# Loads of the last stage behind the overflow block's weights, one input copy less

## What is computed

```python
u = rmsnorm(h, norm_ffn)
# top-1 group of 4, top-2 of the 4 experts in it: 2 of 16 experts per token
for e in range(N_EXPERTS):
    gu = jnp.einsum('bld,df->blf', u, w_gate_up[e])
    hid = jax.nn.silu(gu[..., :D_EXPERT]) * gu[..., D_EXPERT:]
    moe = moe + combine[..., e:e + 1] * jnp.einsum('blf,fd->bld', hid, w_down[e])
h = h + moe
u = rmsnorm(h, norm_ple)
gate = jax.nn.sigmoid(jnp.einsum('bld,de->ble', u, w_ple_gate))
h = h + gate * jnp.einsum('blp,pd->bld', p_l, w_ple_proj)
# then a final RMSNorm
```

## Time and profile before

| what | value |
|---|---|
| runs | 850.77, 850.83, 851.63 us, median 850.83 us |
| the profiled execution | 849.0 us, span 847.2 us |
| mean granted clock of PE | 0.994 |
| busy: PE, DVE, ACT, POOL | 822.9, 385.5, 215.2, 152.6 us |
| moved by DMA | 135.31 MB |

### The profile page before, as it was taken

One profiled execution on the slowest core, in us unless ns is written; L12 is line 12 of the kernel. 1 busy time (PEld: TensorE's weight loads), 2 busy tenths in 40 slices (PEclk: granted clock), 3 DMA queues, 4 the chain that ended last, 5 costly groups with the idle time before them and its releaser, 6 DMA issues. The chain is left out here.

```text
span 847.2 us, 13448 instructions
## 1 busy us (share of the span) xinstructions
PE 822.9 (97%) x5462; PEld 519.9 (61%) x5462; DVE 385.5 (46%) x857; ACT 215.2 (25%) x464; POOL 152.6 (18%) x184
## 2 busy tenths in 40 slices
PE   8999999999999999999999999999999999979996
PEld 4546777888889987777777775455343333334452
DVE  3223556676646522664852559546441111105543
ACT  3202153258223311131001101123031111114554
POOL 0234420014054133300220052001000000004000
PEclk9999999999999999999999999999999999989999
DMA  9420344402020110522252024005899999966111
GB/s 361 193 99 25 133 150 163 155 1 108 1 101 4 45 58 13 198 72 99 100 198 100 1 100 178 25 26 209 352 415 417 427 421 420 406 279 198 50 38 50
DMA packets 19197, 135.31 MB, mean 160 GB/s; under 512 B 2496, under 2 KB 3136, under 8 KB 11712
## 3 DMA queue, kind: packets, MB, share of 16 engines
q1 hardware_dynamic: 11888, 104.33, 31.2%
q0 software_dynamic: 4896, 24.48, 7.8%
q10 hardware_dynamic: 2352, 5.64, 2.0%
HBM read 119.01 MB, written 19.63 MB: 164 GB/s over the span
## 5 line engine op out<-in xcount | busy, mean ns | idle before, releaser
L765 PE MATMUL pair<-mem 128*128 128x288 f32 x640 | 158.9, 408 | 0.0
L765 PEld LDWEIGHTS pair<-mem 128*128 128x128 f32 x640 | 120.3, 190 | 35.6 <-ACT mem L1381 2.1
L935 PE MATMUL single<-mem 128*128 128x288 f32 x448 | 110.0, 407 | 0.3
L935 PEld LDWEIGHTS single<-mem 128*128 128x128 f32 x448 | 84.7, 190 | 25.7 <-issue 1.6
L1275 PE MATMUL single<-mem 128*32 128x512 f32 x768 | 85.1, 594 | 1.1 <-DVE mem L2304 0.9
L1381 ACT ACTIVATE mem<-single 128x256 f32<-128x256 f32 (+5 forms) x111 | 45.6, 421 | 134.7 <-PE single L1181 48.7
L1381 ACT ACTIVATE mem<-pair 128x512 f32<-128x512 f32 (+5 forms) x77 | 33.5, 485 | 156.7 <-PE pair L765 63.0
L1360 PE MATMUL pair<-mem 128*128 128x512 f32 (+1 forms) x192 | 63.3, 524 | 0.0
L1275 PEld LDWEIGHTS single<-mem 128*32 128x32 f32 x768 | 24.0, 110 | 52.7 <-issue 51.6
L2297 DVE SCALAR_TENSOR_TENSOR mem<-single,mem 128x256 f32<-128x256 f32 x12 | 5.8, 484 | 104.3 <-PE single L1275 91.4
L1172 PE MATMUL pair<-mem 128*128 128x512 f32 x112 | 51.0, 601 | 0.0
(11 more groups left out here) (407 smaller groups left out, 1135.2 us busy)
## 6 DMA issues: line engine op xcount, KB each, us to landing
mem<-in_w_gu SPq DMA_DIRECT2D x17, 2048.0 KB, 14.8
mem<-in_w_down SPq DMA_DIRECT2D x17, 1024.0 KB, 14.9
y_slots<-mem SPq DMA_DIRECT2D x12, 512.0 KB, 11.1
y_slots<-in_zeros POOLq DMA_DIRECT2D x8, 512.0 KB, 7.8
mem<-in_w_ga SPq DMA_DIRECT2D x2, 2048.0 KB, 7.6
mem<-in_w_gb SPq DMA_DIRECT2D x2, 2048.0 KB, 7.6
mem<-in_w_wo SPq DMA_DIRECT2D x2, 2048.0 KB, 7.7
mem<-in_w_pg SPq DMA_DIRECT2D x2, 2048.0 KB, 14.1
```

The lines of the kernel that those rows point to most:

```text
L765: last = nc.tensor.matmul(pb[:, hf, 0:HALF], w(k), rhs[:, k, hf * HALF:(hf + 1) * HALF], start=(k == 0), stop=(k == kk - 1))
L935: last = nc.tensor.matmul(single[plan.buf[s]][:, 0:HALF], lhs[:, k, :], rhs[:, k, :], start=(k == 0 and j in (0, 1, 3, 4)), stop=(k == 3), ...
```

## The change

The load of `w_pg0` and that of `w_proj` are taken out of SP's loop over phases. Both are issued behind the overflow block's pair of loads, with the load of `pT` between them, which moves from POOL's queue to SP's. The second copy of the last columns of `pT` goes away, and with it the two waits and the view that it had; tile 4 reads the first copy. `w_proj` and `pT` share the semaphore `ld_p`, on which PE waits once, for both.

```diff
-        pT4 = view(BLK + 17408, 2, 64)
...
-                if p == NPH - 2:
-                    sp.dma_start(view(BLK, CHUNK_W), a["w_pg0"]).then_inc(sem("w_pg"), 16)
                 if p:
                     store(p - 1)
                 for e in range(NEXP - 4):
                     if last_phase(e) == p - 1:
                         load_dn(e + 4)
-                if p == NPH - 3:
-                    sp.dma_start(w_proj.rearrange("p k c -> p (k c)"), a["w_proj"]).then_inc(sem("w_proj"), 16)
...
                     sp.dma_start(w_gu_flat[0], a["w_gu"][bass.ds(e * P, P), :]).then_inc(sem("ov_w"), 16)
                     sp.dma_start(w_dn_flat[0], a["w_down"][bass.ds(e * P, P), :]).then_inc(sem("ov_w"), 16)
+            sp.dma_start(w_proj.rearrange("p k c -> p (k c)"), a["w_proj"]).then_inc(sem("ld_p"), 16)
+            sp.wait_ge(sem("xT_mm"), NPH)
+            sp.dma_start(pT, a["pT"]).then_inc(sem("ld_p"), 16)
+            sp.dma_start(view(BLK, CHUNK_W), a["w_pg0"]).then_inc(sem("w_pg"), 16)
             store(NPH - 2)
...
-            pe.wait_ge(sem("ld_p"), 16)
-            pe.wait_ge(sem("w_proj"), 16)
+            pe.wait_ge(sem("ld_p"), 32)
...
-                if t == 4:
-                    pe.wait_ge(sem("ld_p"), 32)
...
-                            last = nc.tensor.matmul(pair[t % 2][rows, hf, cols], pT[:, k, t * P:t * P + n] if t < 4 else pT4[:, k, :],
+                            last = nc.tensor.matmul(pair[t % 2][rows, hf, cols], pT[:, k, t * P:t * P + n],
...
-            pool.wait_ge(sem("xT_mm"), NPH)
-            pool.dma_start(pT, a["pT"]).then_inc(sem("ld_p"), 16)
...
-            pool.wait_ge(sem("ld_p"), 16)
-            pool.dma_start(pT4, a["pT"][:, :, 4 * P:TOK]).then_inc(sem("ld_p"), 16)
```

## The result

| | before | after |
|---|---|---|
| median | 850.8 us (12 runs, 848.07 to 852.69) | 852.95 us (12 runs, 851.16 to 854.39) |
| ratio to before | | 1.0028, 95% interval 1.0017 to 1.004 |
| profiled execution, span | 849.0, 847.2 us | 853.86, 852.0 us |
| busy PE | 822.9 us | 825.1 us |

The change made the kernel slower by 0.28%: 2.4 us by the ratio, while the two medians are 2.15 us apart. The forecast was 849.6 us in a range from 847.5 to 851.6. The before column holds twelve runs; the median of 850.83 us that the forecast started from is that of three of them.

The account below looks back on a forecast made before the run. The prediction took PE as the bound, with time to regain only at its 4.09 us wait for the overflow weights and the clock fall behind it. Terms -2.7 + 1.5 = -1.2 us gave 849.6 us, range 847.5 to 851.6.

Parts of the forecast that it names:

- Step 1: Overflow pair lands by 742.7, its products start 3.6 us earlier, and PE finishes the projections at 764.25 to 765.95, was 770.80.
- Step 2: Loads moved behind the overflow pair land later but stay hidden; w_proj and pT have 3.5 us to spare.
- Step 3: SP's queue has a hole from 730.6, later bytes shift, and phase 11's store lands at 759.4 instead of 756.5.
- The prediction's other estimate for this store: Phase 11's store, by the skill page's DMA figures: the 10.03 MB would be in at 757.6.
- Step 4: POOL's gathers: removed copy saves 1.07 us; phase 11's store releases POOL, gathers issued from 759.5 instead of 760.97.
- Step 5: Last stage: h3 ready at 768.1, PE waits 2.2 to 3.9 us, transposes (L1344, later L1340) start 2.7 us earlier.
- Step 6: Behind PE's wait for h3: the clock falls to half for 3.4 us, on uncovered work, costing 1.5 us.
- D: Overflow stores on ACT's queue meet a full SP queue and release POOL late: +3.6 us, 854.4; chance 0.10.
- C: Queue makes up for its hole, h3 arrives just behind PE: -4.7 us, 846.1; chance 0.08.
- B: Rival: PE waits for h3, clock stays up, 848.1 us, chance 0.30. In positions (B + 20.05): start of overflow block's transposes.
- E: Overflow pair still lands after 745.5 through late drain or SP; PE's wait only shrinks: 850.8 us; chance 0.07.

Follow-up runs that it names:

- fifth run: Changed kernel with the overflow pair ahead of the store of phase 9, the wait between its loads naming phase 10's down products: 855.31 us, ratio 1.0078.
- eleventh: Changed kernel, w_pg0 back in SP's loop, phase 11's store ahead of w_pg1, w_pg1 and norm_final after the first tile's gathers, PE's gate-weight wait split: 845.29 us, ratio 0.9961.
- eighth run: Kernel before with only the second copy of pT's last columns taken away: 849.46 us, ratio 1.0001.
- fourth: Changed kernel with the second copy of pT's last columns put back on POOL's queue and read by tile 4: 852.37 us, ratio 1.0027.
- tenth run: Kernel before with only the overflow pair issued ahead of the store of phase 9, behind w_pg0: 848.21 us, ratio 0.9983.
- third run: Changed kernel with six extra unused products keeping PE busy while it waits for h3: 850.12 us, ratio 0.9999.
- second run: Changed kernel with the stores of phases 10 and 11 issued ahead of w_pg0 and w_pg1: 852.43 us, ratio 1.0032.
- sixth: Changed kernel with both stores ahead of the gate weights, and SP waiting for PE's first projection before w_pg0, w_pg1 and norm_final: 854.04 us, ratio 1.0048.
- first: Changed kernel with the load of w_pg0 back in SP's loop, in phase 10: 846.96 us, ratio 0.9962.
- ninth: Changed kernel with the overflow pair ahead of the store of phase 9, the wait between its loads set one phase sooner, to phase 9: 847.66 us, ratio 0.9977.
- seventh: Changed kernel with w_pg0 back in SP's loop and the store of phase 11 ahead of w_pg1: 849.05 us, ratio 0.9994.

## Why the prediction was wrong

**What held.** Step 1: the pair's first load landed 7.6 us after its issue, PE's wait went, the products took 1.96 us (1.9 forecast), the projections 14.00 (14.0), and PE was done with them at B + 20.05 (B + 19.9 to 21.6 forecast). Step 2: `w_proj` and `pT` were hidden; `pT` landed at 750.6, 12.5 us after its issue, and PE asked for it at 753.06. The margin was 2.4 us and not 3.5, and it ran out in the fifth run, where these loads were late (PE waited 0.78 us for `pT`), and by 0.24 us in the eleventh. The kind of the result was foreseen too: a wait for `h3` in place of the old one, and a low clock behind it. What failed is the size of three terms, and they carried it over zero.

**Step 3, the queue's end, was the largest.** Forecast: the store of phase 11 in at B + 15.1 (759.4 - 744.31). Measured: B + 17.5 (764.53 - 747.01). Of these 2.4 us, 1.3 lie in a sentence that I took for certain, "their issue stays at 732.60". SP issued the pair 3.59 us after the store of phase 9, where it had been 2.33, so it came at B - 10.4 instead of B - 11.7. The other 1.1: the 7.93 MB behind the first load took 20.3 us and not 19.2. That would be 390 GB/s, but the queue was not that slow. It moved 8.21 MB in these 20.3 us (744.22 to 764.53), 404 GB/s, so that some 0.7 us went to bytes that the sum didn't have ahead of that store, those of `norm_final` and of the overflow block's stores, and 0.4 to the rate. The hole's cost thus came to 5.4 us against the kernel before (B + 17.5 to B + 12.15), where the sum had 2.9. The prediction's other estimate for this store, 757.6 (B + 13.3), was further off.

**Step 4.** I had POOL issue 0.1 us after that store. It took 0.81, and the same 0.75 of issue stands behind the release in every chain that I read there, whichever store gives it. The step also let the overflow stores land in 1.5 us as on an idle queue, while by step 3's own sum the queue was full until 760.7; that they took up to 8.1 us didn't show in the time, as the other store was later still. What the removed copy saved is real (the eighth run), but that issue time is not part of it, and in the changed kernel the copy is hidden (the fourth).

**Step 5.** From the first gather to L1340 it was 7.94 us, and 8.6 forecast, the one term that erred in the other direction. With steps 3 and 4 (3.1 late) L1340 came at B + 26.3 and not at B + 23.8. The 2.7 us of gain were 0.2.

**Step 6.** I took one stretch of half clock of 3.4 us, at 1.5 us. The granted clock of the changed kernel:

```profile
771.00:771.50 0.50, 0.00 (x0) 0.00 (x0) 0.00 (x0) 0.00 (x0) 0.00 (x0) 0.86 1.08 352
...
778.00:778.50 0.50, 0.50 (x6) 0.03 (x2) 0.50 (x1) 0.00 (x0) 0.00 (x0) 0.81 0.05 8
```

It fell at 771.4, 4.3 us after PE's last product, and came back at 778.2: 6.8 us at 1.2 GHz, twice the 3.4 of the kernel before. The wait went on for 1.9 us behind the fall, so 4.9 us of it lie on work. That the long wait made the stretch long is not shown: in the tenth run the clock fell 1.1 us after PE was back at work, and it too was at half for 6.8 us. The cost, L1340 to L1356, is 5.24 - 2.84 = 2.4 us. The third run shows that it is all of the loss. So -0.2 + 2.4 = +2.2 us stands where I had -2.7 + 1.5.

**The rivals.** D was half right. Its mechanism was there: the overflow stores took 6.1 to 8.1 us and not 1.5, and the last landed at about 763.5, 1.1 us ahead of the gate that I had forecast. The second run shows them alone as the gate, the sixth that an empty queue gives the 1.5 us back. But my price, 11.5 us from a gather of 128 KB, was too high, and I treated the two gates as rivals when they open together: both wait for the loads to run out. I then set the store's term alone against the clock, without asking what happens when both are late. In D I put the change's slower side at a gather issue beyond 762.8, which is B + 18.5; the measured one was B + 18.3, and with 2.4 us of clock instead of 1.5 that was already past the point. C, the queue making up for its hole, had nothing for it. B's condition was sound, though its time was not: behind waits of 2.67 and 2.90 us, which lie inside the 2.2 to 3.9 that I forecast, the clock stayed up (first and ninth runs). E came true in its first half, as SP got to the pair 1.3 us later, but the pair was still in ahead of PE's need.

**What stays open.** SP's 1.3 us. From the store of phase 9 to the pair it is 2.33 us in the kernel before and in the eighth run, 3.09 to 3.27 in the first, seventh and eleventh, which have `w_pg0` alone in the loop, and 3.56 to 3.59 in the changed kernel and the other runs with neither load there (second, third, fourth, sixth). The number goes with how many of the two loads stand in SP's loop, but which property of SP does that was not tried. It also stays open why the last overflow store took 5 to 7 us in the runs in which the queue was only about half full by then.

## What to carry to other kernels

Moving a load back in a full queue is free only if something takes its place at once; if the next transfers in program order wait for a computed result, the queue runs dry, and here everything behind came later by that hole, small stores and the releases hung on them above all. Look for a transfer that can fill the hole (here the load that was taken out of it) before looking at its order, and price every release that waits for the last byte, not only the one that came last in the old profile. And a wait that is moved to a place ahead of work that nothing covers can be paid twice: in its length and, where it is long enough for the clock to fall (here 3.30 us and more, but not 2.67 or 2.90), in the clock behind it.

## What was not expected of the hardware

A store of 32 KB on ACT's queue landed in 1.5 us when SP's queue was idle or nearly so, and in 5 to 9 us when it was loaded with weights (last store of the four: 1.5, 5.3, 6.6, 8.1 and 9.3 us in the sixth, first and seventh runs, the changed kernel and the second run). The Trainium skill, "DMA: Bandwidth & Descriptors", section "Queues, rings and completion order", says that an engine takes its queue rows in turn, a packet at a time; the runs agree that a neighbour queue delays, and give what it costs here. The prediction counted four turns for the four stores. By the trace of the changed kernel they are 192 packets, 12 for each of the 16 DMA engines, and the packets of the weight loads hold 16 KB, 0.65 us each at a sixteenth of the 404 GB/s. One of those ahead of each of the 12 gives 7.8 us for all four stores, an estimate from these numbers; 9.7 us passed from the first one's issue to the last one's landing. No run tested it. In the same way, gathers of 512 KB took 4 to 5.6 us with no loads beside them and 13.9 beside 4.7 MB of loads (sixth run).

The granted clock stayed at 1.00 through idle times of 2.67 and 2.90 us ahead of the last stage (first and ninth runs). It was at half behind those of 4.09 (before) and 6.22 us (after), and products were slow behind the 3.30 us of the tenth run and the 3.75 us of the seventh as well (there the eight transposes took 1.63 us, not 1.04). In these two the granted clock was still at 1.00 when PE went back to work, and fell 1.1 and 0.4 us later.
